# A two-layer model on one core: the Hyena filter network, its norms and half sums placed between the projection's tiles, and the transposes of z moved

## Time and profile before

| what | us |
|---|---|
| median of three runs (4004.02 to 4009.92) | 4004.97 |
| the profiled execution, as timed | 4006.81 |
| its span, first to last instruction | 4005.0 |
| of it, PE busy / DVE busy / ACT busy | 3440.0 / 1111.7 / 597.9 |
| 12 tiles of the Hyena projection, on PE | 714.87 to 799.34 |
| from there to the end of the inverse transform on PE | 799.34 to 955.64 |

### The profile page before, as it was taken

One profiled execution on the slowest core, in us unless ns is written; L12 is line 12 of the kernel. 1 busy time (PEld: TensorE's weight loads), 2 busy tenths in 40 slices (PEclk: granted clock), 3 DMA queues, 4 the chain that ended last, 5 costly groups with the idle time before them and its releaser, 6 DMA issues. The chain is left out here.

```text
span 4005.0 us, 47547 instructions
## 1 busy us (share of the span) xinstructions
PE 3440.0 (86%) x20976; PEld 1672.6 (42%) x20976; DVE 1111.7 (28%) x1921; ACT 597.9 (15%) x1164; POOL 7.5 (0%) x36
## 2 busy tenths in 40 slices
PE   6988998869897877777777799998999986999998
PEld 3567886323344322222222244444444434444443
DVE  1246665132013000000000023663566114122210
ACT  2133231010002100000000021143212003021100
POOL 0000000000000000000000000000000000000000
PEclk9989999979996999999999999999999997999999
DMA  6243334311220599999999902111433325212120
GB/s 222 69 170 129 130 127 175 33 45 32 65 98 23 217 421 421 420 421 421 419 421 421 409 25 84 42 43 48 122 116 128 107 49 205 68 63 84 63 87 34
DMA packets 228147, 668.66 MB, mean 167 GB/s; under 512 B 37144, under 2 KB 100956, under 8 KB 177125
## 3 DMA queue, kind: packets, MB, share of 16 engines
q1 hardware_dynamic: 226952, 665.25, 44.3%
q10 hardware_dynamic: 989, 0.36, 0.0%
HBM read 640.97 MB, written 22.31 MB: 166 GB/s over the span
## 5 line engine op out<-in xcount | busy, mean ns | idle before, releaser
L2533 PE MATMUL banks<-h_T,weight_ring 128*128 128x512 f32 x1408 | 613.2, 596 | 6.2 <-PEq L89 6.2
L1972 PE MATMUL banks<-weight_ring,xe_T 128*64 128x512 f32 x2048 | 468.9, 600 | 148.7 <-DMA weight_ring<-in_exp_w 146.5
L2533 PEld LDWEIGHTS banks<-h_T,weight_ring 128*128 128x128 f32 x1408 | 267.6, 191 | 338.2 <-issue 338.2
L1972 PEld LDWEIGHTS banks<-weight_ring,xe_T 128*64 128x64 f32 x2048 | 143.0, 137 | 464.2 <-issue 258.4
L1752 PE MATMUL banks<-weight_ring,ffn_act 128*128 128x512 f32 x704 | 306.1, 598 | 14.5 <-PEq L2683 7.5
L1987 PE MATMUL banks<-weight_ring,hid_T 128*64 128x512 f32 x1024 | 236.6, 605 | 84.7 <-DMA weight_ring<-in_exp_w 83.8
L2592 DVE SCALAR_TENSOR_TENSOR conv<-banks,cols,conv 128x510 f32<-128x510 f32 (+1 forms) x176 | 131.8, 749 | 342.7 <-ACT conv L2562 338.1
L1752 PEld LDWEIGHTS banks<-weight_ring,ffn_act 128*128 128x128 f32 x704 | 135.0, 192 | 185.6 <-issue 185.6
L2041 DVE TENSOR_TENSOR hid<-silu,banks 128x1024 f32<-128x1024 f32 x16 | 19.5, 1221 | 663.0 <-issue 566.6
L582 PE MATMUL banks<-h_T,weight_ring 128*128 128x512 f32 x416 | 184.0, 602 | 22.0 <-PEq L89 22.0
L1987 PEld LDWEIGHTS banks<-weight_ring,hid_T 128*64 128x64 f32 x1024 | 71.8, 138 | 248.9 <-issue 143.4
(11 more groups left out here) (552 smaller groups left out, 3759.6 us busy)
## 6 DMA issues: line engine op xcount, KB each, us to landing
weight_ring<-in_exp_w SPq DMA_DIRECT2D x192, 2048.0 KB, 11.2
weight_ring<-in_ada_w SPq DMA_DIRECT2D x24, 2048.0 KB, 9.0
weight_ring<-in_ffn_w_up SPq DMA_DIRECT2D x44, 1024.0 KB, 6.7
weight_ring<-in_mod_w SPq DMA_DIRECT2D x12, 2048.0 KB, 8.5
weight_ring<-in_ffn_w_down SPq DMA_DIRECT2D x10, 2048.0 KB, 7.8
weight_ring<-in_attn_w_in SPq DMA_DIRECT2D x7, 2048.0 KB, 7.9
weight_ring<-in_w_in SPq DMA_DIRECT2D x6, 2048.0 KB, 13.1
weight_ring<-in_w_in SPq DMA_DIRECT2D x9, 1024.0 KB, 7.9
```

The costliest lines, as they stand in the source:

```text
L1972: mm = pe.matmul(k.ps[64 * half:64 * half + 64, 2 * c + b % 2, :], xeT[:, kt, e * CAP:(e + 1) * CAP], w[:, r, 512 * b:512 * b + 512], star ...
L2533: mm = pe.matmul(k.ps[:, b + c, :], w[:, c, kt, m * P:m * P + P], hT[:, kt, :], start=kt == 0, stop=kt == 7)
```

The seven small loads, which stood behind the window, the Fourier matrices and the inverse, now come straight behind the stores of `gain_rows`. The diff, cut to its core:

```diff
@@ weight_chunks
-    out += [[(I["k_window"].rearrange("(k p) n -> p k n", p=P), [P, 4, 512])]]
@@ hyena
-def hyena(k, u, hy):
+def hyena(k, hT, hy):
...
+    per_tile = {2: filters[0:2], 3: filters[2:4], 4: filters[4:6], 5: filters[6:8]}
...
+        ztok, sumdif, prod, scr, window = u[:, 4:8, :], filt, filt, absum, spec[:, 0, :, :]
...
-            sync.wait_ge(loads, 16 * 7)
-            k.ring.load_ahead(sync, 3)
+            sync.dma_start(window, I["k_window"].rearrange("(t p) n -> p t n", p=P)).then_inc(window_landed, 16)
+            k.ring.load_ahead(sync, 5)
+            sync.wait_ge(loads, 16 * 7)
...
+            for i in range(TILES):
+                project(i)
+                if i == 0:
+                    pe.wait_ge(loads, 16 * 7)
+                    ev(("mlp", 0), pe.matmul(k.ps[0:64, 1, :], w1[:], feat[:], start=True, stop=True))
+                if i == 1:
+                    pe.wait_ge(act_done, act_n[("sine", 0)])
+                    ev(("mlp", 1), pe.matmul(k.ps[0:64, 3, :], w2[:], hid[:], start=True, stop=True))
+                if i == 2:
+                    pe.wait_ge(act_done, act_n[("sine", 1)])
+                for t, d in per_tile.get(i, ()):
+                    if t:
+                        pe.wait_ge(dve_done, dve_n[("filter", t - 1, d)])
...
+                if 3 <= i < 7:
+                    for n in (2 * i - 6, 2 * i - 5):
+                        pe.wait_ge(act_done, act_n[("abs", *filters[n])])
...
+            pe.wait_ge(dve_done, dve_n[("z", HY_T - 1)])
+            for t in range(LT):
+                pe.wait_ge(act_done, act_n[("spectrum", 0, t)])
+                for j in range(HY_T):
+                    mm = pe.transpose(k.ps[:, order[t], j * P:j * P + P], u[:, 8 + j, t * P:t * P + P], k.sq("eye"))
+                ev(("turned", t), mm)
+            pe.wait_ge(act_done, act_n[("turned", LT - 1)])
...
-            pe.wait_ge(dve_done, 19)
             for j in range(HY_T):
-                for c in range(2):
-                    for kt in range(LT):
+                for kt in range(LT):
+                    if j == 0:
+                        pe.wait_ge(dve_done, dve_n[("prod", max(kt, j))])
+                    for c in range(2):
...
+                if 7 <= i < 11:
+                    t = i - 7
+                    link(dve.tensor_tensor(scr[:, 0, :], filt[:, 1, t, :], filt[:, 0, t, :], ALU.subtract))
+                    link(dve.tensor_tensor(sumdif[:, 0, t, :], filt[:, 0, t, :], filt[:, 1, t, :], ALU.add))
+                    ev(("sumdif", t), dve.tensor_copy(sumdif[:, 1, t, :], scr[:, 0, :]))
+                if i == 7:
+                    ev("inverse", dve.reciprocal(inv_norm[:], k.ps[:, 1, :]))
+                if i >= 8:
+                    ev(("z", i - 8), dve.tensor_tensor(u[:, i, :], u[:, i, :], u[:, i - 4, :], ALU.mult))
...
-    k.ring.done(3)
+    k.ring.done(5)
@@ first_layer
-                with sbuf(nc, "hyena_u", [P, 12, L], F32) as u:
-                    project_with_shifts(k, k.hT, 12, k.col("hy_conv_w", 0, 36), k.col("hy_conv_b", 0, 12),
-                                        lambda i: u[:, i, :], None, (), 3)
-                    hyena(k, u, hy)
+                hyena(k, k.hT, hy)
```

More of the change, by code:

```diff
@@ L685, in _, with project @@
-            dft = k.ring.chunk(1).rearrange("p (c t n) -> p c t n", c=2, t=LT)
-            pe.wait_ge(dve_done, 15)
-            pe.wait_ge(act_done, 14)
+            ev = counter(pe_done, pe_n)
+            def project(i):
+                j, m = i // 4, i % 4
+                if m == 0:
+                    k.ring.wait(pe, j)
+                w = k.ring.chunk(j).rearrange("p (k n) -> p k n", k=8)
+                if i >= 4:
+                    pe.wait_ge(dve_done, dve_n[("sums", i - 4)])
+                for kt in range(8):
+                    mm = pe.matmul(k.ps[:, bank(i), :], w[:, kt, m * P:m * P + P], hT[:, kt, 0:L], start=kt == 0, stop=kt == 7)
+                ev(("tile", i), mm)
@@ L710, in _ @@
                                        start=(c, kt) == (0, 0), stop=(c, kt) == (1, LT - 1))
[L711 removed]
+                ev(("y", j), mm)
         @block.scalar
         def _(act):
[L715 to L723 removed]
@@ L724, in _ @@
-            for t in range(LT):
-                act.wait_ge(pe_done, 11 + t)
-                act.activation(ztok[:, t, :], k.ps[:, t, :], ACT.Copy).then_inc(act_done, 1)
-            for n in range(8):
-                act.wait_ge(pe_done, 23 + n)
-                act.activation(spec[:, n // 4, n % 4, :], k.ps[:, n % 8, :], ACT.Copy).then_inc(act_done, 1)
+            ev = counter(act_done, act_n)
+            for i in range(TILES):
+                act.wait_ge(pe_done, pe_n[("tile", i)])
+                if i % 4 == 3:
+                    act.sem_inc(k.ring.used, 1)
+                ev(("middle", i), act.activation(u[:, i, :], k.ps[:, bank(i), :], ACT.Identity,
+                                                 scale=taps[:, TILES + i:TILES + i + 1], bias=bias[:, i:i + 1]))
+                if i < 2:
+                    act.wait_ge(dve_done, dve_n[("sine", i)])
+                    ev(("sine", i), act.activation(hid[:], arg[:], ACT.Sin))
+                for t, d in per_tile.get(i, ()):
+                    act.wait_ge(dve_done, dve_n[("filter", t, d)])
+                    if t:
+                        act.wait_ge(pe_done, pe_n[("norm", 2 * t + d - 2)])
+                    ev(("abs", t, d), act.activation(absum[:, d, :], filt[:, d, t, :], ACT.Abs))
@@ L731, in _ @@
+            for c in range(2):
+                for kt in range(LT):
+                    act.wait_ge(pe_done, pe_n[("spectrum", c, kt)])
+                    ev(("spectrum", c, kt), act.activation(spec[:, c, kt, :], k.ps[:, (1, 3, 5, 7, 0, 2, 4, 6)[4 * c + kt], :], ACT.Copy))
+            for t in range(LT):
+                act.wait_ge(pe_done, pe_n[("turned", t)])
+                ev(("turned", t), act.activation(ztok[:, t, :], k.ps[:, (1, 3, 5, 7)[t], :], ACT.Copy))
         @block.vector
@@ L733, in _ @@
             link = Chain(dve, linked)
-            dve.wait_ge(loads, 16 * 7)
-            for i in range(2):
-                dve.wait_ge(pe_done, 1 + i)
-                link(dve.tensor_scalar(arg[:], k.ps[0:64, i, :], fcol[:, i:i + 1], fcol[:, 2:3], ALU.add, ALU.mult))
-                wrapped_sine(dve, None, link, arg[:], arg[:], tmp[:])
-                dve.sem_inc(dve_done, 1)
-            k.ring.wait(dve, 0)
-            window = k.ring.chunk(0)[:, 0:LT * HY_W].rearrange("p (t n) -> p t n", t=LT)
@@ L755, in _ @@
[L755 to L765 removed]
+            done = []
```

161 lines of the change are left out of this document (85 added, 76 removed).

## The result

The changed kernel takes 3973.06 us (median of 4 runs, 3969.22 to 3976.05), the kernel before 4007.44 us beside it (4 runs, 4004.02 to 4019.95). The ratio, worked out from all these runs, is 0.9903 with a 95% interval of 0.9887 to 0.9919. Applied to 4007.44 that is 38.9 us less, between 32.5 and 45.3; the two medians alone differ by 34.4. The same kernel measured a second time gave 0.9894 (0.9865 to 0.9923). So it is faster by 1%, clear of the noise. The mechanism is the one that was forecast, but the gain is smaller than the 44.8 us of the forecast, and the time lies 5 us above the range.

A forecast was written before the change was run, and what follows sets the result against it. PE, by its work or its waits for short DVE and ACT chains, bounds 714 to 956 us. Removing 73.6 us and adding 28.8 gives 44.8 less: 4005.0 to 3960.2, said as 3960; range 3948 to 3968.

The forecast's parts named there:

- The step with 4.6 + 1.8 for the first output tile: Inverse transform's start: taking products in turn removes the 4.56 us pause (4.6) and keeps the upper clock (1.8).
- The edits at nothing: Hyena stage: sines, DVE's fullest tile, ACT's work, window and Fourier loads cost PE 0; second sine up to 0.5 us.
- C: Rival: clock drops in the wait for loads and stays low among the interleaved products; 4049 us, chance 0.02.
- B: Rival: more small waits or clock dips on PE's path, about 2.2 us per dip; 3964 to 3967, chance 0.16.
- D: Rival: nothing gained, freed time given back later by weight loads; about 4003 us, chance 0.02.
- A: Rival: small loads aren't held up by the stores, so 7.7 + 2.3 go; 3950 us, chance 0.17.
- the wait for the small loads: Behind projection tile 0: PE waits 7.7 us for loads queued behind six stores; bounds no wait and 9.8.
- 730.1 plus about 1.2 of their own: Small loads' landing: last store lands at 730.1, loads about 1.2 us later, so PE waits until 731.3.
- The clock behind the wait: After the wait for small loads: lower clock, first network product included, costs 2.3 us.
- Their row gives them the same duration: Filter products between tiles: 64 rows last as long as 128, 0.86 us each; 18 small products make 15.5.
- small waits appear behind each group of filter products: Sign that would show the forecast wrong, in PE's timeline among the projection tiles; no size given.
- the transposes with their wait: Between the filter's and z's spectra: 16 transposes 2.4 us plus 0.9 wait for ACT's last copy, 3.3 in all.

The follow-up runs named there:

- six kernels: The changed kernel, its repeat, and four edits of it: loads on ACT's queue, all products awaited, transposes first, half sums late; PE waits 8.67 to 13.63 us.
- late stores: Changed kernel with the six small gain stores issued behind the small loads and the window, not ahead of the stage: 3937.05 us, ratio 0.9817.
- the padding: Late stores with the filter products' 64 rows padded to 128 with zeros: 3939.89 us, ratio 0.9836.
- the three kernels where no store holds it: Changed kernel with the gain stores behind the loads (0.9817), that with filter products padded (0.9836), and the kernel before with its stores moved later (0.9968).

## Why the prediction came out as it did

**Right, by its own steps.** What the change takes away: z's spectrum and everything from it to the end of the stage has no pause longer than 0.90, as said, and from tile 2 on the clock is at 1.00. (The dense passes between the two waits are 176 + 36 + 64; the "192 + 36" of the prediction counts tile 0 in and the filter's spectrum out.) The step with 4.6 + 1.8 for the first output tile was measured alone at 6.5. The edits at nothing cost nothing: neither sine nor DVE's full tile 7 held PE (174.19 us of work in 175.10). The half sums behind tile 11 would have cost 13.8; so their cover is real. C, where the clock stays low among the small products, is out: it was up again within tile 1, which took 9.04 us instead of 6.87. For its fear, and B's, that products of 64 rows don't bring the upper clock, the prediction had one row, in which PE also stood idle for 3.5 of 17.5 us; which of the two kept the clock at 0.50 there, no run tells. D is out too, since the 37.5 us at 980 us are 37.6 at the end. A is out by the table above.

**The term that was mis-sized** is the wait for the small loads, with the clock behind it. The step that failed is "730.1 plus about 1.2 of their own": it took the landing of the last load behind the last store as one short transfer. It is 3.0 us here (0.9 to 3.9 over six kernels), and the wait 9.34, not 7.7: 1.6 more. Nor was 9.34 a bad draw: the six waits are 8.67 to 13.63. The upper bound of 9.8 that the step itself gave holds four of them, but not 10.10 and 13.63. The clock behind the wait cost 2.8 and not 2.3: the first network product and tile 1 took 10.86 us (736.68 to 747.54), and 8.06 in late stores, where no wait comes before them (699.15 to 707.21). That is 0.5 more.

**The term that wasn't there** is the change of form. "Their row gives them the same duration" was read from eight filter products one behind the other, with one change of form at each end; placed in pairs between tiles, every pair brings two. The prediction put this at nothing on the strength of that row. Tiles 2 to 6 with all that stands among them take 49.74 us (748.54 to 798.28), against 5 x 6.87 + 16 x 0.86 = 48.1: 1.6 more, of which the padding took 1.57 away. The two network products bring their changes too: the first with tile 1 takes 8.06 at the upper clock (late stores) where the sum had 7.73, the second 1.00 where it had 0.86. That is 0.5, and 2.1 in all. That "small waits appear behind each group of filter products" was a sign of being wrong that the prediction had named itself.

**The term that was too large** is the transposes with their wait: 1.91 + 0.90 = 2.8 instead of 3.3. Here the rule on transposes was weighed against a row. z's spectrum took 27.73 us against 27.63 for the other two, so it started at the upper level. The Trainium skill ("TensorE: Matmul & The Clock Gate", Part 4) says that transposes don't engage the full clock; the forecast that it would start low, made from that rule, did not come true here. But no run here shows a clock that has to rise behind transposes in this place, only one that stays up: the question between the rule and the earlier trace rows was not put again.

In the stretch this is 1.6 + 0.5 + 2.1 - 0.5 = 3.7 us, and the stretch gained 240.77 - 199.54 = 41.2 where the forecast had 44.8, so 3.6 are missing; the rest is rounding.

**The stage start** made as much again. The sum took it for granted that all ahead of tile 0 stays as it is. On average it does about that (713.5 over the six kernels of the table with the stores ahead), but a single execution shows it between 710.51 and 718.55, and the profiled one of the changed kernel is the latest of seven: 3.7 us. That is bad luck. But the row with the explanation was there: tile 0 starts 1.11 us behind the end of SP's last store issue. The idleness of 19.21 us ahead of tile 0 was read in the prediction, for the clock, but not followed to its cause.

**From the span to the median.** For the profiled execution the forecast is 3960.2 + 1.8 = 3962.0, and it took 3969.22, which is 3.6 + 3.7 = 7.3 with rounding. It is the fastest of its four; their median is 3.8 higher, which is chance too. And the 1.8 between 4006.81 and 4004.97 was given away when the sum was set against the median of three runs; the same kernel had medians of 4007.44 (4 runs), 4012.96 (13) and 4004.93 (7) later. As a ratio the forecast was 0.9888, just inside the interval of 0.9887 to 0.9919. So of the 12.9 us between 3960.2 and 3973.06, 3.6 are wrong terms of the sum, 3.7 the start of the stage in one execution, and 5.6 the distance from that execution to a median. With a base that spreads over 4001 to 4020 us, and whose medians lie 8 us apart, plus or minus 2 for "dips in later stages" was too narrow.

## What to carry to other kernels

Before a stage's start is moved or a load is put at its start, look at what the DMA engines still have in flight from the stage before: here six stores of 4-byte elements delayed the loads issued behind them, on SP's queue and on ACT's alike, so such stores belong behind the loads that PE wants first. An idle time ahead of the stretch under change is a part of the change's environment: follow it to the instruction that ends it, here SP's issue of those stores. Small matmuls with fewer active rows between full tiles are cheap but not free; charge both changes of form.

## What was not expected of the hardware

- Six stores of 1024 elements (4 KB each) hold SP's queue for 23.7 to 27 us at the end of the stage, and the last lands 25.1 to 27 us behind its issue. Moved behind the small loads they still take 15.6 us to issue (696.06 to 711.63), but nobody waits.
- The last load on ACT's queue was announced 13.5 us behind the end of its issue, where the same load takes 3.3 with nothing ahead of it. For some 5 us of that (723 to 728.5) the DMA engines were nearly idle.
- A change from 128 active rows to 64 or back costs 0.195 us, twice for each pair of filter products between tiles.
- A pause of 9.34 us brought the clock to its lower level, and one of 4.58 us cost the inverse 1.8 us; one of 3.41 us ahead of 16 transposes cost nothing.

Open: why the loads come 0.9 us behind the last store in one execution and 3.9 in another; why the stores' issues take 24 us in one and 27 in another; what moves PE's work ahead of the Hyena stage, which started at 690.60, 694.83 and 707.23 in the three kernels where no store holds it. The last would need many profiles of one kernel.
